# Down products of two feed-forward parts as seven block products, with the sums of blocks made by GpSimd

## The reference

```python
def swiglu_half(x, pre, post, w_gate, w_up, w_down):
    h = rmsnorm(x, pre)
    y = (jax.nn.silu(h @ w_gate) * (h @ w_up)) @ w_down
    return x + 0.5 * rmsnorm(y, post)

def layer(...):
    h = swiglu_half(x, ...ffn1...)
    u = rmsnorm(h, mix_pre);  p = u @ w_in      # three branches follow
    ...
    y = swiglu_half(h, ...ffn2...)
```

## Time and profile before

| | us |
|---|---|
| median of 3 runs | 3128.83 |
| lowest, highest | 3127.26, 3136.36 |
| the profiled execution | 3137.18 |
| its span | 3135.5 |
| mean granted TensorE clock | 0.981 of full |
| TensorE matmul busy | 2997.9 |
| VectorE, ScalarE, GpSimd busy | 1674.7, 1183.5, 346.8 |

### The profile page before, as it was taken

How to read it: one execution, slowest core, us unless ns; L and a number is a source line. 1 busy time by engine, 2 the same in 40 slices (tenths; PEclk the granted TensorE clock), 3 DMA queues, 4 the chain that set the end, 5 groups by cost and what they waited for, 6 DMA issues and landing times. The chain is left out here.

```text
span 3135.5 us, 63709 instructions
## 1 busy us (share of the span) xinstructions
PE 2997.9 (96%) x26970; PEld 2836.4 (90%) x26970; DVE 1674.7 (53%) x2830; ACT 1183.5 (38%) x2244; POOL 346.8 (11%) x356
## 2 busy tenths in 40 slices
PE   8999999999999988878899989999998999999998
PEld 8999999999999978838777569999998999999998
DVE  7655554554545556566554552343425755565453
ACT  5333334553112233244665351221243433334444
POOL 3000000112001123230003000000015100000111
PEclk9999999999999999989999999999998999999999
DMA  6222237663422120011015641112123222225764
GB/s 173 82 72 73 80 102 230 205 193 108 142 71 68 48 89 4 18 27 45 13 46 166 221 169 51 51 44 61 31 77 99 82 82 82 75 82 176 222 186 138
DMA packets 419542, 312.53 MB, mean 100 GB/s; under 512 B 45720, under 2 KB 391105, under 8 KB 418490
## 3 DMA queue, kind: packets, MB, share of 16 engines
q1 hardware_dynamic: 414394, 288.98, 30.6%
q0 software_dynamic: 3824, 19.47, 1.8%
q10 hardware_dynamic: 1040, 0.00, 0.0%
HBM read 249.20 MB, written 59.21 MB: 98 GB/s over the span
## 5 line engine op out<-in xcount | busy, mean ns | idle before, releaser
L2033 PE MATMUL banks<-hid_pieces,dn_part 128*128 128x344 f32 x3168 | 501.9, 320 | 2.0 <-DVE dn_part L1998 1.3
L2033 PEld LDWEIGHTS banks<-hid_pieces,dn_part 128*128 128x128 f32 x3168 | 498.3, 188 | 3.0 <-DVE dn_part L1998 1.7
L1802 PE MATMUL banks<-x_pieces,gate_pieces 128*128 128x258 f32 x3360 | 414.3, 283 | 0.0
L1802 PE MATMUL banks<-x_pieces,up_pieces 128*128 128x258 f32 x3360 | 414.1, 283 | 0.0
L1802 PEld LDWEIGHTS banks<-x_pieces,gate_pieces 128*128 128x128 f32 x3360 | 408.6, 189 | 0.0
L1802 PEld LDWEIGHTS banks<-x_pieces,up_pieces 128*128 128x128 f32 x3360 | 408.6, 189 | 0.0
L1167 PEld LDWEIGHTS banks<-XR,pR 128*128 128x128 f32 (+1 forms) x1800 | 284.2, 188 | 10.3 <-issue 6.1
L1167 PE MATMUL banks<-XR,pR 128*128 128x344 f32 (+1 forms) x1800 | 289.6, 322 | 3.6 <-DVE pR L2509 2.9
L2012 DVE TENSOR_TENSOR dn_part<-dn_raw,dn_part 128x768 fp32r<-128x768 f32 (+1 forms) x188 | 173.7, 938 | 217.4 <-ACT dn_part L2006 217.4
L1167 PE MATMUL banks<-XR,mg_gate 128*128 128x344 f32 x1728 | 283.3, 319 | 1.3 <-PEq L53 1.3
L1167 PEld LDWEIGHTS banks<-XR,mg_gate 128*128 128x128 f32 x1728 | 273.8, 188 | 1.6 <-issue 1.6
(11 more groups left out here) (523 smaller groups left out, 4744.2 us busy)
## 6 DMA issues: line engine op xcount, KB each, us to landing
dn_raw<-in_ffn_down SPq DMA_DIRECT2D x94, 384.0 KB, 3.5
dn_raw<-in_ffn_down SPq DMA_DIRECT2D x94, 320.0 KB, 3.2
hid_spill<-h_stage SPq DMA_DIRECT2D x44, 516.0 KB, 3.4
hid_raw<-hid_spill SPq DMA_DIRECT2D x24, 688.0 KB, 4.9
praw<-in_w_in SPq DMA_DIRECT2D x24, 512.0 KB, 4.2
sq<-in_w_in SPq DMA_DIRECT2D x24, 512.0 KB, 4.1
tiles<-h_spill SPq DMA_DIRECT2D x8, 1376.0 KB, 8.7
gu_raw<-in_ffn_gate SPq DMA_DIRECT2D x20, 512.0 KB, 4.0
```

The lines of the kernel that those rows point to most:

```text
L1802: ins = k.nc.tensor.matmul(out, self.w[m][:, a, w, f * P:(f + 1) * P], self.x[p][:, b, x, f * TQ:(f + 1) * TQ], start=first and f == 0 and ...
L2033: ins = k.nc.tensor.matmul(k.ps[j][:, 0:TG], w[a][:, f * P:(f + 1) * P], k.hid_pieces[h][:, b, f, :], start=h == 0 and f == 0 and r == 0, ...
```

## The change

The product with w_down is cut in 2 x 2 x 2 blocks: output features 0 to 511 and 512 to 1023 (the first index of A), hidden blocks with even and odd numbers, token halves of 516 (the second index of B). Seven block products take the place of eight. Four of them use sums: S1 to S4 of weight blocks, T1 to T4 of activation blocks. GpSimd makes these during gate and up, one chain for each pair of hidden blocks and kind: it loads from DRAM, adds, and stores the sums in DRAM (`w_sums`, `t_sums`), from where they are loaded like weights and activations. In the diff k, P, DT and FT are the kernel's own names (P = 128, DT = 8, FT = 22).

```diff
-    HID_PARTS = ((0, 4), (4, 8), (8, 11))
+    H_PARTS = ((0, 0, 5), (0, 5, 9), (0, 9, 11), (1, 0, 6), (1, 6, 11))
     DN_PARTS = ((0, 6), (6, 11))
+    DOWN = (("A11", "B11"), ("A12", "B21"), ("S2", "T2"), ("S3", "T3"), ("A22", "T4"), ("S1", "T1"), ("S4", "B22"))
+    FRESH = (0, 2, 3, 5)
+    UNITS = [(m, j, (0, 1)) for m in range(6) for j in range(4)] + [(6, j, (q,)) for q in range(2) for j in range(4)]
+    LOADED = 28
...
+    def load_hidden(self, sp, m, i):
+        q, a, b = self.H_PARTS[i]
+        x = self.DOWN[m][1]
+        if x[0] == "T":
+            self.sums_stored(sp)
+            src = self.k.t_sums[:, int(x[1]) - 1, a:b, q * TQ:(q + 1) * TQ]
+        else:
+            odd = int(x[1] == "2")
+            src = self.k.hid_spill[:, 2 * a + odd:2 * b:2, self.hid_cols(x, q)]
+        self.hid_landed[i].done(sp.dma_start(self.k.hid_raw[m % 2][:, q, a:b, 1, :], src))
 
...
+        m, j, _ = self.UNITS[u]
+        x = self.DOWN[m][0]
+        if x[0] == "S":
+            return self.k.w_sums[:, int(x[1]) - 1, a:b, j * P:(j + 1) * P]
+        at = 4 * P * (x[1] == "2") + j * P
+        return self.dn_src[:, 2 * a + int(x[2] == "2"):2 * b:2, at:at + P]
+
...
+    def unit_done(self, eng, u):
+        self.dn.wait(eng, 2 * u + 2 if u < 24 else u + 25)
...
+        self.hid_stored.wait(sp, 2 * it)
+        for i in range(2):
             self.load_hidden(sp, 0, i)
         self.product[4].wait(sp, self.last - 4)
+        self.load_hidden(sp, 0, 3)
+        self.load_down(sp, 1)
+
+    def sp_down(self, sp, between):
+        self.hid_stored.wait(sp, 2 * self.N - 1)
+        self.load_hidden(sp, 0, 2)
+        self.load_hidden(sp, 0, 4)
+        self.product[4].wait(sp, self.last - 3)
+        self.load_down(sp, 2)
+        self.load_down(sp, 3)
+        self.store_hidden(sp, self.N - 1, 1)
+        self.hid_stored.wait(sp, 2 * self.N)
+        self.load_down(sp, 4)
+        self.unit_done(sp, 1)
+        for i in (2, 3):
+            self.load_hidden(sp, 1, i)
+        self.chain_sums.wait(sp, 2 * self.CHAIN)
+        self.load_hidden(sp, 1, 4)
+        for u in range(5, self.LOADED):
+            self.unit_done(sp, min(u - 3, 23))
+            self.load_down(sp, u)
+            m = (u - 2) // 4
+            if 6 <= u < 26 and u % 4 in (2, 3):
+                for i in ((0, 1, 2) if u % 4 == 2 else (3, 4)):
+                    self.load_hidden(sp, m + 1, i)
             between(sp, u)
...
```

`load_down` waits for the stored sums where its weights are an S, `sp_down_ahead` loads parts 0, 1 and 3 of the first activation block. The chain:

```diff
+    def chain(self, pool, i, kind):
+        k, nc = self.k, self.k.nc
+        x, y, z = ((t[:, 0:4 * P] if kind == "S" else t) for t in k.chain_slots)
+        s, (yz, xs) = self.chain_sums, self.chain_stored
+        at = s.n
+        even, odd, low, high = 2 * i, 2 * i + 1, slice(0, 4 * P), slice(4 * P, 8 * P)
+        one, two = slice(0, 2 * TQ), slice(2 * TQ, T)
+        src = {"S": [(even, high), (odd, high), (even, low), (odd, low)], "T": [(even, two), (even, one), (odd, two), (odd, one)]}
+        whole = self.dn_src if kind == "S" else k.hid_spill
+        src = [whole[:, f, c] for f, c in src[kind]]
+        out = (k.w_sums if kind == "S" else k.t_sums)[:, :, i, :]
+        for t in self.chain_stored:
+            t.wait(pool, t.n)
+        for dst, a in zip((x, y, z), src):
+            self.chain_landed.done(pool.dma_start(dst, a))
+        self.chain_landed.wait(pool, self.chain_landed.n)
+        s.done(nc.gpsimd.tensor_tensor(y, x, y, ALU.add if kind == "S" else ALU.subtract))
+        s.wait(pool, at + 1)
+        yz.done(pool.dma_start(out[:, 0, :], y))
+        s.done(nc.gpsimd.tensor_tensor(x, z, x, ALU.subtract))
+        s.wait(pool, at + 2)
+        xs.done(pool.dma_start(out[:, 2, :], x))
+        if kind == "S":
+            s.done(nc.gpsimd.tensor_tensor(z, y, z, ALU.subtract))
+        else:
+            s.done(nc.gpsimd.tensor_tensor(z, z, y, ALU.subtract))
+        s.wait(pool, at + 3)
+        yz.done(pool.dma_start(out[:, 1, :], z))
+        xs.wait(pool, xs.n)
+        self.chain_landed.done(pool.dma_start(x, src[3]))
+        self.chain_landed.wait(pool, self.chain_landed.n)
+        s.done(nc.gpsimd.tensor_tensor(x, x, z, ALU.subtract))
+        s.wait(pool, at + 4)
+        xs.done(pool.dma_start(out[:, 3, :], x))
+
+    def chains(self, pool):
+        for i in range(self.N):
+            self.hid.wait(pool, 8)
+            self.chain(pool, i, "S")
+            self.hid_stored.wait(pool, 2 * i + 2)
+            self.chain(pool, i, "T")
...
```

```diff
+    def unit_pe(self, pe, u, between):
...
+        s = self.slot(u)
+        for q in quarters:
+            if m:
+                self.evicted(pe, m - 1, j, q)
+            for i, (first, end) in enumerate(self.DN_PARTS):
+                if u < self.LOADED:
+                    self.dn_low.wait(pe, 2 * u + i + 1)
+                for f in range(first, end):
+                    for part, (hq, a, b) in enumerate(self.H_PARTS):
+                        if j == 0 and (hq, a) == (q, f):
+                            self.hid_low.wait(pe, 5 * m + self.h_order(m).index(part) + 1)
+                    for r, (a, b) in enumerate(((k.dn_high, 0), (k.dn_high, 1), (k.dn_parts, 0))):
+                        ins = k.nc.tensor.matmul(k.ps[2 * j + q][:, 0:TQ], a[s][:, f * P:(f + 1) * P],
+                                                 k.hid_pieces[m % 2][:, q, f, b, :],
+                                                 start=m in self.FRESH and f == 0 and r == 0,
+                                                 stop=f == self.HALF - 1 and r == 2, skip_group_check=True)
             self.dn.done(ins)
+            if u == 0 and q == 0:
+                self.fourth(pe, self.last)
+            between(pe, u, q if u < 24 else 1)
...
+    def evict_act(self, act, u):
+        k, (m, j, quarters) = self.k, self.UNITS[u]
+        for q in quarters:
+            self.dn.wait(act, self.count(u, q))
+            at = (1 - m) * 2 * TQ + q * TQ
+            self.out.done(k.nc.scalar.activation(k.A[:, j, at:at + TQ], k.ps[2 * j + q][:, 0:TQ], ACT.Copy))
+
+    def evict_dve(self, dve, u):
+        k, (m, j, quarters) = self.k, self.UNITS[u]
+        for q in quarters:
+            self.dn.wait(dve, self.count(u, q))
+            if m == 2:
+                self.evicted(dve, 0, j, q)
+            elif m < 5:
+                self.evicted(dve, 2, j, q)
+            else:
+                self.evicted(dve, 3 if m == 5 else 2, j, q)
+            first, second = slice(q * TQ, (q + 1) * TQ), slice((2 + q) * TQ, (3 + q) * TQ)
+            twelve = k.A[:, j, second]
+            out, to = {2: (twelve, twelve), 3: (k.A[:, 4 + j, second], twelve), 4: (k.A[:, 4 + j, first], twelve),
+                       5: (k.A[:, 4 + j, second], k.A[:, 4 + j, second]), 6: (twelve, twelve)}[m]
+            self.out_dve.done(k.nc.vector.tensor_tensor(out, to, k.ps[2 * j + q][:, 0:TQ], ALU.add))
+
+    SQUARES = [(0, f) for f in range(DT)] + [(g, f) for f in range(4, DT) for g in (1, 2)] + [(g, f) for g in (1, 2) for f in range(4)]
...
```

```diff
             def between(sp, u):
-                if u in (5, 12, 20):
-                    mid.fetch_group(sp, (5, 12, 20).index(u))
-                if u == 32:
-                    mid.spill(sp, 0)
-                if u == 42:
-                    proj.first_loads(sp)
+                if u == 6:
+                    mid.fetch_group(sp, 0)
 
             ffn1.sp_down(sp, between)
+            mid.fetch_group(sp, 1)
+            proj.first_loads(sp)
+            mid.spill(sp, 0)
+            ffn1.unit_done(sp, 28)
+            mid.fetch_group(sp, 2)
             ffn1.done(sp)
             proj.load_shift(sp)
...
+            def between(pe, u, q):
+                if (u, q) in ((20, 0), (28, 1)):
+                    post.add_up(pe, u // 28)
+                if (u, q) in ((20, 1), (29, 1)):
+                    post.spread(pe, u // 29)
+                if (u, q) == (23, 0):
+                    mid.dve_s.wait(pe, ("norm", 0, DT - 1))
...
             def between(act, u):
-                g, at = u // 16 - 1, u % 16
-                if g >= 0 and at == 2:
-                    post.root(act, g)
-                if g >= 0 and at == 6:
-                    mid.high(act, g, range(0, 4))
-                if g >= 0 and at == 7:
-                    mid.high(act, g, range(4, DT))
-                if u in (45, 46):
-                    proj.high(act, u - 45)
+                if u in (20, 29):
+                    post.root(act, u // 29)
+                if u in (23, 24):
+                    mid.high(act, 0, range(4 * (u - 23), 4 * (u - 22)))
+                if u in (29, 30):
+                    ffn1.unit_done(act, 27)
+                    proj.high(act, u - 29)
+                if u == 31:
...
             x.constants_ready(dve)
 
             def between(dve, u):
-                g, at = u // 16 - 1, u % 16
-                if g >= 0 and at == 2:
-                    post.inverse(dve, g)
-                for first, n, step in ((0, 3, 3), (3, 6, 4), (6, 8, 5)):
```

(16 more changed lines are left out.)

403 lines of the change are left out of this document (208 added, 195 removed).

## The result

| | before | after |
|---|---|---|
| median, us | 3132.60 | 3232.69 |
| lowest, highest | 3127.26, 3141.91 | 3229.98, 3252.67 |
| profiled execution, its span | 3137.18, 3135.5 | 3234.39, 3232.6 |
| mean granted TensorE clock | 0.981 | 0.957 |

The changed kernel takes 1.033 of the time of before, 95% interval [1.028, 1.038]: **slower by 100 us**, where 3091 us and a gain of 37 had been forecast. It is the course of rival (b), to which I had given a chance of 0.12.

The account below looks back on a forecast made before the run. TensorE, busy 96% of the span, was taken as the bound. 2 x (-26.8 + 2 + 1 + 2.5 + 2) + 1 = -37.6 us took 3137.18 to 3099.6, and 8.4 us to the median gave 3091 us, range 3075 to 3125.

Parts of the forecast that it names:

- rival (b): Late chains, from 20.6 us each, hold SyncE's wait ahead of unit 5's loads in down; 3187 us at 22; chance 0.12.
- the 3.0 us for a transfer: GpSimd's chains: each 256 KB DMA transfer takes 3.0 us, ends 2.1 and 4.5; four in series per 18.8 us chain.
- the break-even of 20.6: Chains beside gate and up: at 20.6 us a chain, lateness at unit 4 of down uses up the gain.
- rival (a): Somewhat late chains, 19.7 to 20.6 us, make TensorE stand at unit 4 of down; 3091 to 3128 us; chance 0.13.
- the budget of 19.7: Gate and up: 21 chains have 19.7 us each between the plain hidden blocks and the last hidden block's store.
- Matmuls: Down: 1848 matmuls of 258 columns at 120.4 ns replace 1584 of 344 at 157.4; -26.8 us in each part.
- Norm sum of group 0: Down, after the first quarter of unit 20: TensorE waits for GpSimd's addition; +2.5 us each part, ends 0 and 5.
- Entry: Start of down: the first block's even hidden rows land late behind other loads; +1 us each part, ends 0 and 4.
- VectorE beside the chains: Gate and up: GpSimd additions block VectorE operations with two SBUF inputs; +2 us each part, ends 0 and 22.
- Last chain: Down, unit 4: the last chain's sums can't be hidden behind gate and up; +2 us each part, ends 0 and 8.
- Tail: End of the first part: VectorE ends group 1's norm and lows behind TensorE's last unit; +1 us once.
- Rival (d): Down's smaller matmuls miss 120 ns because weight loads show; nothing won from 135 ns on, 3128 us; chance 0.03.

Follow-up runs that it names:

- Experiments 8 and 9: Changed kernel, SyncE's gate and up weight loads from the second iteration cut to an eighth, and to half: 3159.25 us (1.0071), and 3176.33 us (1.0135).
- experiment 4: Changed kernel with a fourth tile (slot) for the chains, so all four loads are issued at a chain's start: 3113.91 us, 0.9911 of before.
- experiment 1: Changed kernel without any chains; down reads plain blocks of the same shapes in place of sums: 3099.43 us, 0.9882 of before.
- Experiment 5: Four-slot kernel with the norm sum of group 0 moved half a unit later on TensorE in both parts: 3104.65 us, 0.990 of before.
- experiment 6: Four-slot kernel with moved norm sum, plus the second quarter's hidden-block cut moved from block 6 to 9: 3108.03 us, 0.9908 of before.
- experiment 7: Changed kernel, three slots, each chain moving and adding half of the columns: 3113.50 us, 0.9924 of before.
- 2: Changed kernel with only 16 of the 22 chains of each part made, other rows read instead: 3097.72 us, 0.9875 of before.

## Why the prediction was wrong

**The step that failed** is the 3.0 us for a transfer, with the sentence that charged nothing for the new DMA traffic beyond it. Four transfers on a chain's path took 15.8 us in the first part, not 12.0, and a chain 22.9 us, past the break-even of 20.6, so that SyncE and TensorE waited for the last sums:

| term | predicted | measured, mean | with SyncE idle |
|---|---|---|---|
| third load, issue to addition | 3.0 | 4.74 | 3.7 to 4.1 |
| store, issue to fourth load | 3.0 | 3.76 | 2.7 |
| fourth load | 3.0 | 3.87 | 3.2 to 3.6 |
| last store to next chain | 3.0 | 3.40 | 2.9 |
| an addition | 1.5 | 1.3 to 1.5 | 1.27 |
| hand-over from addition to own store | 0.08 | 0.30 | 0.30 |
| period | 18.8 | 22.9 | 18.8 to 19.6 |

The means are over all 22 chains of the first part. Undisturbed, the chain takes what I forecast to within 5%, though its terms are not the forecast ones. The 2.7 us behind the store are not the store's: in them GpSimd issues it (0.56), makes the third sum (1.28) and issues the store of that (0.30 + 0.56), and then issues the fourth load without a wait. Experiments 8 and 9 show most of what disturbs the chain. The prediction had both halves in hand and didn't join them: it read the triplets of 256 KB at 4.5 us and a DMA share of 0.27 that the chains would bring to some 0.6, and against rival (a) it wrote "nothing else loads the queues". In the changed kernel the share is 0.54 in this stretch of gate and up, twice the 0.28 of before:

```profile
100.00:200.00 100.00, 100.00 (x833) 100.00 (x833) 71.08 (x110) 34.68 (x66) 44.51 (x53) 1.00 0.54 172
```

The Trainium skill's 2.0 us plus bytes/436 GB/s (DMA: Bandwidth & Descriptors, Anatomy of one DMA) give an estimate of 2.6 us for 256 KB. The trace agrees for stores, 2.4 us in the median, and not for loads, 3.5 and 3.7; and neither this nor my 3.0 us has a term for other traffic.

**What was right in that step** is the rest of its arithmetic. At 22.9 us a chain and with the budget of 19.7 the last sums are 21 x 3.2 = 67 us late, in each part, and by the prediction's own rule for rival (b) the profiled execution would take 3099.6 + 134 = 3234 us; it took 3234.39. So near a hit is luck in part. The budget was a little larger: with four slots, where GpSimd waits for the hidden blocks, the last chain began 423.3 and 422.4 us after the first (experiment 4), 20.1 us a chain. In the changed kernel it was 480.0 and 481.7, that is 57 and 59 us late. Against experiment 1 TensorE waited 59 and 65 us more for hidden pieces in down, and 10 us are matmuls that took longer, which the rule didn't have. My margin was 0.9 us in 18.8, on a term whose own bounds were 15.2 and 24.8. The ends lay on both sides of break-even, and the row that I called nearest was chosen with 0.12 left for the other side. The range even left rival (b) out.

**The other terms**, by the runs:
- *Matmuls*, -26.8 us: right. Without chains 1287 matmuls took 155.06 us, 120.5 ns each, where 120.4 was forecast. Down is 19.5 and 17.8 us shorter there than before, and the terms that apply without chains leave more, -26.8 + 1 + 2.5 = -23.3; the next two terms were too small.
- *Norm sum of group 0*, +2.5 us: 2.7 in the changed kernel, 3.9 and 3.7 in experiment 1. Experiment 5 shows that most of the wait can be had back.
- *Entry*, +1 us: too small. TensorE waits 1.7 us for the first weights and 2.5 for hidden pieces (experiment 1, first part), against 0.7 in all before, so +3.5 us, inside the ends of 0 and 4; in the changed kernel the first is 3.0 to 3.6.
- *VectorE beside the chains*, +2 us in each part: in both parts together TensorE waited 0.2 us for it in gate and up of the changed kernel, 2.6 us with twenty chains, 3.5 with four slots, 3.2 in experiment 6. So 4 us were too much, and the upper end of 22 in each part was far off; more on it below.
- *Last chain*, +2 us: hidden in the changed kernel behind the 60 us. In experiment 5 it is 3.1 us in the first part (1.83 + 1.23) and 4.9 in the second (two waits, the longer 4.24).
- *Tail*, +1 us once, charged in the first part: not seen, for the stretch between the parts is shorter in every changed kernel, by 0.1 to 9.7 us. Behind the second down product it is 20.9 against 20.4 us.
- *Rival (d)* was priced wrongly. At 135 ns a matmul the 26.8 us are gone in each part and the other terms stay, which gives 3091 + 53.6 = 3145 us; the 3128 belongs to about 130 ns. Nothing hung on it, since the matmuls took 120.5.

**Not in the sum at all:** the clock in and behind the idle stretch. The windows around it in the second part, all engines:

```profile
2950.00:3010.00 60.00, 0.00 (x0) 0.00 (x0) 0.00 (x0) 0.00 (x0) 27.99 (x36) 0.52 0.39 128
3010.00:3030.00 20.00, 16.84 (x113) 16.57 (x114) 10.68 (x11) 11.63 (x18) 0.00 (x0) 0.75 0.92 287
3030.00:3110.00 80.00, 80.00 (x670) 80.00 (x669) 41.72 (x51) 30.82 (x40) 3.92 (x3) 1.00 0.60 183
```

While TensorE stood the granted clock was at 0.52, that is near the lower of its two levels (1.2 of 2.4 GHz); it was at 0.75 in the 20 us in which matmuls began again, and at 1.00 behind them. The 113 matmuls of these 20 us took 149 ns each, 3 us more in all than at 120.4. The same 1848 matmuls and their neighbours kept TensorE busy for 235.9 and 232.8 us in the two down products, against 228.3 and 230.7 without chains: 7.6 and 2.1 us. With twenty chains, at a third of the idle time, it is 7.4 and 3.4, so the cost doesn't grow with the length of the idle. Nor does it need a long one: in experiment 7 the longest wait at unit 4 was 4.4 us in the first part, and the clock was still 0.83 in the 20 us around it (520 to 540), with 106 matmuls of 142 ns. The busy time of the two down products together lies between 459.0 and 465.1 us in the six runs without a long idle (experiments 1, 2 and 4 to 7), and between 466.1 and 469.8 in the four with one.

## What to carry to other kernels

A price for a transfer has to be read in the traffic that it will meet. When work is given to a queue that looks idle, add up what the other queues carry in the same stretch, and take the nearest row in such company, not the nearest in size. When a serial chain of small transfers has to fit a budget, and the bounds of its length lie on both sides of break-even, being late deserves more than the 0.12 that I gave it, however good the middle looks; and the first thing to try is a further buffer, so that loads and stores of neighbouring links overlap. Here one tile of 258 KB took the chain's own time from 19.3 to 13.3 us and turned a loss of 3.3% into a gain of 0.9%.

## What was not expected of the hardware

- GpSimd needs 0.30 us from the end of its own operation to the issue of a DMA that waits for it, in every run with chains, where 0.08 us had been read from a square to an addition, and about 0.6 us from the landing of its last store to the next issue (in the chain of waits: landing at 2984.55 + 2.30 = 2986.85, issue at 2987.43).
- Loads of 256 KB took 3.5 to 3.7 us, stores of the same size 2.4, on the same queue. At 128 KB loads took 2.4 to 2.6 and stores 2.0 to 2.8. Three of a chain's four loads are issued together; the fourth, alone with SyncE idle, took 3.09 to 3.23 us in the last three chains of the changed kernel.
- VectorE's subtraction of 1024 columns in gate and up took 1.22 us without chains, 1.41 to 1.98 in the mean of a group beside them. From 200 to 300 us, experiment 1 and then the changed kernel (last figures: busy us, mean ns):

```profile
L1986 DVE TENSOR_TENSOR sq<-sq,banks 128x258 f32<-128x258 f32 x30 | 12.7, 422 | 14.6 <-PE banks L1893 14.6
...
L1840 DVE TENSOR_TENSOR up_pieces<-gu_raw,up_pieces 128x1024 fp32r<-128x1024 f32 x3 | 3.7, 1218 | 0.0
```

```profile
L1986 DVE TENSOR_TENSOR sq<-sq,banks 128x258 f32<-128x258 f32 x30 | 12.4, 419 | 6.6 <-PE banks L1893 6.3
...
L1840 DVE TENSOR_TENSOR up_pieces<-gu_raw,up_pieces 128x1024 fp32r<-128x1024 f32 x3 | 5.2, 1718 | 0.0
```

The operation with a PSUM operand keeps its 0.42 us. This is what the Trainium skill says of the port pair that the two engines share (SBUF — State Buffer, Who interferes with whom), and the trace agrees: 422 and 419 ns there, 1218 against 1718 ns for two SBUF operands. What was not expected is that 88 additions in each part held VectorE up like this and cost TensorE so little: VectorE's idle in front of its block totals fell from 14.6 to 6.6 us in these 100, so slack that it had there paid for part of it.
